# A gather ring that shrinks from seven slots to six at gather 301, with one head's query weights kept in the freed slot

## The reference, cut to what matters

```python
x = x + concat[retention(n(x)), short_conv(n(x))] @ w_out
x = x + peer(n(x));   y = rmsnorm(x)

def peer(x):                                  # per token, 8 heads
    q = (x @ wq).reshape(T, 8, 2, 128)        # wq: 1024 x 2048, 1 MB for each head
    s1, s2 = q[:, :, 0] @ keys1, q[:, :, 1] @ keys2        # 128 scores each
    v1, i1 = top_k(s1, 16); v2, i2 = top_k(s2, 16)
    top_s, sel = top_k(v1[..., :, None] + v2[..., None, :], 16)
    eidx = (i1 * 128 + i2)[sel]               # 16 of 16384 experts
    gate = softmax(top_s)
    act = gelu(x . u_tab[eidx])
    return sum(gate * act * v_tab[eidx])
```

## Time and profile before

| | |
|---|---|
| time, median of 3 runs | 2945.81 us |
| the profiled execution's own time | 2945.65 us |
| its span | 2943.8 us |
| around the span (the difference) | 1.85 us |
| DMA read and written | 1205.73 MB, mean 410 GB/s |
| of it the gathers' queue (q0) | 1107.36 MB |
| of it SyncE's queue (q1) | 95.93 MB |
| PE / DVE / ACT / POOL busy | 78% / 71% / 67% / 42% of the span |

### The profile page before, as it was taken

The page is one execution under the profiler, slowest core; times in us unless marked ns, Lnnn a source line. Parts: engine busy times, 40 slices in busy tenths (PEclk is TensorE's granted clock), DMA queues, the critical chain, the costliest instruction groups (busy, mean ns, idle before and its releaser), DMA issues.

```text
span 2943.8 us, 36236 instructions
## 1 busy us (share of the span) xinstructions
PE 2300.3 (78%) x12548; PEld 1804.2 (61%) x12548; DVE 2077.0 (71%) x5143; ACT 1967.8 (67%) x3670; POOL 1240.7 (42%) x1063
## 2 busy tenths in 40 slices
PE   9989898998777768888986887778766667666677
PEld 8878786665555556666665555555555555555555
DVE  3677788675688787777666555788868788865544
ACT  2477666777677677666667776777767666667663
POOL 0234334444334334433344344344454445455553
PEclk9999999999888878999996989898866656766669
DMA  8899999999999999999999999999999999999998
GB/s 340 318 403 404 420 408 411 412 420 420 420 419 417 412 410 404 421 421 419 418 418 404 419 420 421 412 420 418 411 419 410 420 420 416 403 414 416 422 421 361
DMA packets 182055, 1205.73 MB, mean 410 GB/s; under 512 B 21744, under 2 KB 27184, under 8 KB 43504
## 3 DMA queue, kind: packets, MB, share of 16 engines
q0 software_dynamic: 152368, 1107.36, 91.2%
q1 hardware_dynamic: 29264, 95.93, 8.3%
q10 hardware_dynamic: 240, 0.13, 0.0%
HBM read 1198.48 MB, written 4.86 MB: 409 GB/s over the span
## 4 chain that ended last, share of the span: by engine, by line
DMA 38%; DVE 24%; PE 22%; ACT 10%; issue 4%; POOL 1%; DVEq 0%; SPq 0%; ACTq 0%; POOLq 0%
DMA ring<-in_uv,idx 38%; DVE ring L2014 12%; PE expert_sum L1590 9%; ACT ring L1210 5%; PE x_ps L1371 2%; PE mm L1473 2%; ACT weights L1206 1%; POOL ring L950 1%; PE mm L1276 1%; DVE pairs_left L1819 1%; DVE pairs_left L1938 1%; ACT L1190 1%; ACT dots L1190 1%; PE expert_sum L1276 1%; PE x_ps L1276 1%
## 5 line engine op out<-in xcount | busy, mean ns | idle before, releaser
L950 POOL DMA_INDIRECT ring<-in_uv,idx x1054 | 1235.1, 1172 | 1683.8 <-PE expert_sum L1590 1464.1
L1590 PE MATMUL expert_sum<-ident_sb,ring 128*128 128x128 f32 x8192 | 1356.6, 322 | 594.5 <-ACT ring L1210 587.8
L2014 DVE CUSTOM_DVE_ANT_0 ring<-ring,xn 128x1024 f32<-128x1024 f32 x1056 | 1285.0, 1222 | 656.8 <-DMA ring<-in_uv,idx 646.8
L1590 PEld LDWEIGHTS expert_sum<-ident_sb,ring 128*128 128x128 f32 x8192 | 1130.2, 167 | 893.4 <-ACT ring L1210 827.6
L1210 ACT ACTIVATE ring<-ring,weights 128x1024 f32<-128x1024 f32 x1024 | 1176.2, 1149 | 33.3
L1190 ACT ACTIVATE dots<-dots 128x1 f32<-128x1 f32 x1056 | 211.5, 200 | 798.7 <-DVE dots L2014 792.2
L1206 ACT ACTIVATE weights<-dots,gate 128x1 f32<-128x1 f32 x1024 | 301.7, 295 | 37.1
L1473 PE MATMUL mm<-xn_in,stream 128*128 128x416 f32 (+1 forms) x500 | 198.3, 521 | 0.0
L1276 PE MATMUL mm<-stream,xn_in 128*128 128x256 f32 (+1 forms) x640 | 162.0, 387 | 0.0
L1276 PEld LDWEIGHTS mm<-stream,xn_in 128*128 128x128 f32 (+1 forms) x640 | 103.9, 177 | 21.4 <-issue 3.8
L1473 PEld LDWEIGHTS mm<-xn_in,stream 128*128 128x128 f32 x500 | 89.9, 200 | 39.6 <-issue 25.1
(11 more groups left out here) (397 smaller groups left out, 1955.6 us busy)
## 6 DMA issues: line engine op xcount, KB each, us to landing
stream<-in_wq SPq DMA_DIRECT2D x21, 1024.0 KB
ring<-in_uv,idx POOLq DMA_INDIRECT x1054
stream<-in_w_conv SPq DMA_DIRECT2D x16, 1024.0 KB
stream<-in_w_ret SPq DMA_DIRECT2D x16, 1024.0 KB
ring<-in_w_ret SPq DMA_DIRECT2D x6, 1024.0 KB, 12.4
x<-in_x SPq DMA_DIRECT2D x8, 512.0 KB, 10.0
out_y<-xn SPq DMA_DIRECT2D x8, 512.0 KB
stream<-in_w_out SPq DMA_DIRECT2D x3, 1024.0 KB
```

The source lines that it names most:

```text
L950: pool.indirect_dma_start(ring[:, g % RING, :], None, uv, bass.IndirectOffsetOnAxis(ap=rows, axis=0)).then_inc(landed[g % RING], 16)
L1590: ins = pe.matmul(expert_sum[:, c * P:(c + 1) * P], ring[:, g % RING, D + c * P:D + (c + 1) * P], ident_sb[:, :], is_transpose=True, start ...
L2014: dve.tensor_tensor_reduce(u, u, xn[:, t % 2, :], 1.0, 0.0, ALU.mult, ALU.add, dots[:, g % RING:g % RING + 1]).then_inc(dotted, 1)
```

## The change: six slots, one kept weight, and works moved

From gather 301 on (`SMALL_RING` = 43 x 7) the gathers go round slots 0 to 5. `slot_of`, `lap_of` and `same_slot_before` replace `g % RING`, `g // RING` and `g - RING` everywhere. The seventh slot is loaded once with the two halves of head 7's query weights, and the pass of head 7 of groups 1 and 2 reads them there, so these two passes leave `STREAM` (60 entries before, 58 now).

Beside it works move: the four x of group 2 are loaded at gather 301 instead of 333; their squares stand at 319, 328, 337 and 346 instead of 346, 348, 350 and 352; the root at a tile's end stands 6 gathers behind it instead of 3 (but for tiles 0, 3 and the sample); the exponentials of tile 3's last four heads stand at 364 instead of 356; the sample's choices start at 853 and are 13 gathers apart instead of 856 and 9. The number of instructions is the same but for the two streamed loads that go and the one that comes.

```diff
-LATER_AT = {4: (374, 11), 6: (654, 16), 7: (775, 10), SAMPLE: (856, 9)}
+LATER_AT = {4: (374, 11), 6: (654, 16), 7: (775, 10), SAMPLE: (853, 13)}
+SMALL_RING = 43 * RING
+def slot_of(g):
+    return g % RING if g < SMALL_RING else (g - SMALL_RING) % (RING - 1)
+def lap_of(g):
+    return g // RING if g < SMALL_RING else SMALL_RING // RING + (g - SMALL_RING) // (RING - 1)
+def same_slot_before(g):
+    return g - RING if g < SMALL_RING + RING - 1 else g - RING + 1
...
-    return {2: 40, 3: 45, 4: 48}.get(t, first_use_at(2) - 7 + 4 * place(t))
+    return {2: 41, 3: 45, 4: 48}.get(t, first_use_at(2) - 7 + 4 * place(t))
...
-    return {0: mix_at(2) + 16}.get(t, end_of(t) + 3)
+    return {0: mix_at(2) + 16, 3: end_of(3) + 3, SAMPLE: TOTAL + 3}.get(t, end_of(t) + 6)
...
-ON_CHIP = {... if p[2] == (0,) or p[2] == (1,) and p[1] in (2, 3)}
+ON_CHIP = {... if p[2] == (0,) or p[2] == (1,) and p[1] in (2, 3) or p[0] and p[1] == PH - 1}
...
+def exp_at(t, last):
+    return choose_at(last, t) + {(0, 3): 5, (3, 7): 14}.get((t, last), 6)
...  # load_x_ahead
-                yield mix_at(1) + 20 if t == 4 else first_use_at(j) - (26 if t < 5 else 32)
+                yield mix_at(1) + 20 if t == 4 else first_use_at(j) - (26 if t < 5 else 64)
...  # load_consts, SyncE
+                yield SMALL_RING + 1
+                sp.wait_ge(slot_free, SMALL_RING)
+                sp.dma_start(ring[:, RING - 1, :].rearrange("p (b k n) -> p b k n", b=2, k=KC),
+                             wq[2 * PH - 2:2 * PH].rearrange("b p k n -> p b k n")).then_inc(kept_wq_in, 16)
...  # GpSimd
-                    pool.wait_ge(slot_free, g - RING + 1)
+                    pool.wait_ge(slot_free, same_slot_before(g) + 1)
...  # norm, ScalarE
-                yield x_root_at(t) - (0 if t < 2 else (8, 6, 3)[place(t)] if t < 5 else 9 - 2 * place(t))
+                yield x_root_at(t) - (0 if t < 2 else (8, 6, 3)[place(t)] if t < 5 else 36 - 9 * place(t))
...  # queries, TensorE
-                    if m in ON_CHIP and h > 1:
+                    if m in ON_CHIP and j:
+                        pe.wait_ge(kept_wq_in, 16)
+                        weight = [chunks_of([ring[:, RING - 1, s * D:(s + 1) * D]]) for s in range(2)]
+                    elif m in ON_CHIP and h > 1:
```

More of the change, by code:

```diff
@@ L168 @@
     PASSES += [(j, h, GROUPS[j], last_turn_at(j) + 5 + PASS_EVERY * h, 2, 0) for h in range(PH)]
-ON_CHIP = {n: p[1] for n, p in enumerate(PASSES) if p[2] == (0,) or p[2] == (1,) and p[1] in (2, 3)}
+ON_CHIP = {n: p[1] for n, p in enumerate(PASSES) if p[2] == (0,) or p[2] == (1,) and p[1] in (2, 3) or p[0] and p[1] == PH - 1}
 SCORED = {(2, 3, 4): [(2, 0), (4, 2), (3, 7)], (5, 6, 7, SAMPLE): [(5, 0), (7, 2), (SAMPLE, 4), (6, 7)],
@@ L949, in _ @@
                 rows = idx[:, QUADS_IN if t == SAMPLE else t % 5, k:k + 1]
-                pool.indirect_dma_start(ring[:, g % RING, :], None, uv,
-                                        bass.IndirectOffsetOnAxis(ap=rows, axis=0)).then_inc(landed[g % RING], 16)
+                pool.indirect_dma_start(ring[:, slot_of(g), :], None, uv,
+                                        bass.IndirectOffsetOnAxis(ap=rows, axis=0)).then_inc(landed[slot_of(g)], 16)
         @block.scalar
@@ L1122, in exponentials @@
                     n = rows_of(t)
-                    yield choose_at(last, t) + (5 if (t, last) == (0, 3) else 6)
+                    yield exp_at(t, last)
                     act.wait_ge(exp_in, pick(last, t) + 1)
@@ L1182, in _ @@
                 t, k = tile_of(g)
-                d = dots[:, g % RING:g % RING + 1]
+                d = dots[:, slot_of(g):slot_of(g) + 1]
                 if t == SAMPLE and k == 0:
@@ L1204, in _ @@
                 act.wait_ge(gelu_done, g + 1)
-                w = weights[:, g % RING:g % RING + 1]
+                w = weights[:, slot_of(g):slot_of(g) + 1]
                 act.activation(w, d, ACT.Copy,
@@ L1579, in _ @@
                         pe.wait_ge(last_v_in[0], 16)
-                        spread_sum(spread[:, k % 3, :], P, ring[:, g % RING, D:], False, False, range(0, 2))
+                        spread_sum(spread[:, k % 3, :], P, ring[:, slot_of(g), D:], False, False, range(0, 2))
                         pe.wait_ge(last_v_in[1], 16)
-                        spread_sum(spread[:, k % 3, :], P, ring[:, g % RING, D:], False, False,
+                        spread_sum(spread[:, k % 3, :], P, ring[:, slot_of(g), D:], False, False,
                                    range(2, QUADS)).then_inc(slot_free, 1)
@@ L1637, in norm @@
                 dve.wait_ge(x_rooted, r + 1)
+                dve.wait_ge(x_scaled, 2 * r)
                 op(dve.reciprocal(stat[0:n, 9:10], stat[0:n, 10 + place(t):11 + place(t)]))
@@ L1950, in gates @@
                     n, heads = rows_of(t), last - first + 1
-                    yield choose_at(last, t) + 8
+                    yield max(exp_at(t, last) + 3, choose_at(last, t) + 8)
                     dve.wait_ge(exp_done, b + 1)
@@ L2011, in _ @@
                         dve.wait_ge(xn_placed, t - 1)
-                dve.wait_ge(landed[g % RING], 16 * (g // RING + 1))
-                u = ring[:, g % RING, 0:D]
+                dve.wait_ge(landed[slot_of(g)], 16 * (lap_of(g) + 1))
+                u = ring[:, slot_of(g), 0:D]
                 dve.tensor_tensor_reduce(u, u, xn[:, t % 2, :], 1.0, 0.0, ALU.mult, ALU.add,
-                                         dots[:, g % RING:g % RING + 1]).then_inc(dotted, 1)
+                                         dots[:, slot_of(g):slot_of(g) + 1]).then_inc(dotted, 1)
                 advance(programs, g)
```

22 lines of the change are left out of this document (11 added, 11 removed).

## The result

The changed kernel takes 2959.68 us (median; 2958.02 to 2966.92), the kernel before beside it 2946.82 (2943.51 to 2950.26): a ratio of 1.0045, 95% interval 1.0034 to 1.0056. The forecast was 2969 us in 2940 to 2990, slower. The profiled execution has a span of 2957.2 us, 13.4 more than before.

What follows compares the result with a forecast made beforehand. The prediction took the gathers' DMA bytes, at 421 GB/s in quiet stretches, to bound the kernel. Its terms, -2.5 + 31 + 10 + 8 - 23 = +23.5 us on 2945.65, gave 2969 us, range 2940 to 2990.

Steps and rivals of the forecast that it cites:

- The bytes: Head 7's weights: two 1 MB loads go and one comes, at 421 GB/s: -2.5 us.
- The quiet round: Gathers without delays, six slots: round 14.9 us, work on a slot 5.3, issue to landing 9.6, rate 421 GB/s kept.
- The table switches: ScalarE's two table loads around an exponential or root, 28 behind 950 us: 28 + 13 us, three quarters taken, +31 us.
- the edge: Shortest time from a gather's issue to its landing that loses nothing: about 8.8 us, allowing 6.1 us of work without stream.
- the three quarters of the prediction: Share of table-switch delays counted, since some late gathers land on VectorE's free time: 31 us kept.
- Other delays and the restart: TensorE and VectorE delays 10 us, losses in present dips beside table loads 8 us, minus today's 23 us loss.
- The moves: Works spread at group 2's x and tile ends thin out piled delays; already in the sum, +15 us at most if they fail.
- the 23 us: Present loss from 950 to 2900 us, in short dips: 416 GB/s against 421 in quiet stretches.
- The signs: Changed profile: 2400 to 2450 us near 400 GB/s, 420 or 421 slices with switches near 415, VectorE and ScalarE waits grow.
- Five in flight are enough: Six slots: issue to landing can shrink to 5.7 us without loss; 2939 or 2944 us; chance 0.30.
- Every delay costs its full period: Six slots: 2.49 us for each of 28 table switches and 10 other places; 2990 us, +92 at most; chance 0.14.
- The kept load: Head 7's weights in the seventh slot might arrive late, stalling TensorE at gathers 330 and 713; 2945 to 2950 us; chance 0.01.

Runs made afterwards that it cites:

- experiment 4: The kernel before, with head 7's two passes reading another resident array, so two 1.05 MB loads go (wrong choices): 2940.86 us, ratio 0.9980.
- experiment 6: The changed kernel (six slots) with exponentials and roots behind gather 295 replaced by operations needing no table load (wrong values): 2945.64 us, ratio 1.0000.
- experiment 7: The changed kernel with seven slots, head 7's weights streamed, and late exponentials and roots replaced by copies and sums: 2944.87 us, ratio 0.9993.
- experiment 1: The changed kernel with seven slots to the end and head 7's weights streamed as before, leaving only the moved works: 2946.26 us, ratio 0.9997.
- experiment 10: The longer switches: the changed kernel with one more table load and root behind each of 15 exponentials: 2980.77 us, ratio 1.0124.
- experiment 2: The changed kernel with all moved works put back; six slots and kept weights stay: 2961.44 us, ratio 1.0047.
- experiment 5: The changed kernel with five slots from gather 301 in place of six: 3115.65 us, ratio 1.0571.

## Why the prediction was right, and where its sum was off

The sum said +23.5 us and it was +13 (12.9 by the medians, 13.4 by the spans). By its steps:

- **The bytes, -2.5.** Measured -2.8 (experiment 4). DMA bytes are the 1204.7 MB predicted.
- **The quiet round.** 14.9, 5.3 and 9.6 us at 422 GB/s, as predicted: a slot less costs nothing where nothing delays.
- **The table switches, +31.** This term was mis-sized. The cause is the right one: taking the switches away takes 14.0 us from six slots (experiment 6) and 1.4 from seven (experiment 7), so 12.6 of the 13.4 us between the kernel of experiment 1 and the changed one hang on them. But 28 of them cost 14.0, not 31. The step that failed is the edge: 8.8 us, read from one dip that lost 1.1 us. The earlier trace rows has that dip; at that place seven slots have 399 GB/s even without a switch, 391 and 406 with one (the table above), so much of the dip isn't the switch's, and it is no measure of an edge. Five slots show an average of 8.3. With that, and the 5.3 + 2.86 = 8.2 us of work instead of my 8.4, the excess is 8.2 - (14.94 - 8.3) = 1.6 us in stretches without stream and 8.2 - (16.4 - 8.3) = 0.1 in those with it. At the three quarters of the prediction this is 12 x 1.2 + 16 x 0.1 = 16 us, where 14.0 were measured; the windows have 0.95 for the 1.2. This sum was made after the result and no run tested it by itself. That the switches under the stream cost next to nothing is worked out, (14.0 - 12 x 0.95)/16 = 0.16 us each, and wasn't measured by itself. The longer switches fit it: of their 21.1 us the last five took 5 x (2.2 - 0.95) = 6, so the ten before them took 1.5 us each for 1.5 us more, as they would if they stood just at the edge.
- **Other delays and the restart, 10 + 8 - 23 = -5.** Without switches six slots are 0.8 us above seven although they move one load less, so 0.8 + 2.8 = 3.6 us are what all other delays cost through the slot. Each of these two times is known to some 2.6 us (their intervals), so the 3.6 may be nothing or twice as much. The prediction replaced the whole loss of today by a new sum, and most of that loss stayed: even without a switch seven slots keep 416 GB/s behind 950 us, so it isn't the switches'. Whether an eighth slot would win it back wasn't run. One reading behind this term was wrong too: the issue at 1604.32 us in the earlier trace rows came late with no releaser, and not because of TensorE (see the last section).
- **Luck.** The switches were put 18 us too high (31 where they make 12.6 of the difference), and the rest 9 too low (-5 for 3.6). They have nothing to do with each other, and the second cancelled about half of the first; with the first alone the forecast would have been 2978 us.
- **The moves.** They were to thin out the piles in the 23 us. With seven slots they bring 0.2 us, with six at most some 2. The stretch at 1100 us did go from 387 to 406, as predicted, and it is 387 again where they are undone (experiment 2), but its 2 us don't show in the time.
- **The signs.** VectorE waits longer for gathers, as predicted. Of the five slices between 1180 and 2080 us that stood at 420 or 421 one fell to 409 and two by 2 or 3, and two stayed, so this sign came only in part; others fell more (419 to 406). ScalarE's wait for dots was to grow and didn't (557.0 to 558.8 us). The fall of 2400 to 2450 us came about, and experiment 1 shows it to be no evidence.
- **The rivals.** "Five in flight are enough" fell with experiment 5: with five slots the average flight in the quiet stretch was 8.3 us at 394 GB/s. Single flights did shrink to 6.44 us, but not all of them, as this rival wanted. By the Trainium skill's rule ("DMA: Bandwidth & Descriptors", section "Anatomy of one DMA — SWDGE (gpsimd) path") of 2.0 us and the bytes at 436 GB/s, an estimate of 4.4 us, five slots would have lost nothing; the runs are against its use for gathers that follow each other. "Every delay costs its full period" fell too: 0.5 us each. But something like it holds past the edge, where experiment 10 pays 1.4 us for 1.5. The kept load came in time: SyncE issued it at 957.94 us and it landed 12.7 us later, before the pass at gather 330.

In one line: seven slots 2946.3 (experiment 1); no switches 2944.9; the sixth slot with the kept weights, still without switches, 2945.6; with the switches 2959.7. Even with no switch at all the trade would only be even: one load is worth 2.8 us and the slot costs about 3.6. No run here that computes the right result is clearly faster than the kernel before.

What stays open: why a lone late issue costs 0.95 us where its excess over the edge is 1.6, and what makes up the better part of the 23 us that were lost with seven slots too, switches or none.

## What to carry to other kernels

The depth of a ring isn't judged in its quiet stretches, where a slot less costs nothing, but by the longest absence of any engine that works on a slot: here seven slots hid 2.86 us and 4.4 us nearly wholly, and six hid neither. Past the edge each further microsecond was paid almost in full, so a slot and a stall are traded against each other: taking a slot is only cheap once the stalls are gone. Find the edge by running with too few slots, not by reading one dip; a single stretch of 50 us varies by some 10 GB/s between kernels of the same time.

## What the runs showed of the hardware that was not expected

GpSimd now and then issues a gather late without anyone to wait for. Timeline of the kernel of experiment 1, transposes and issues:

```profile
2157.93 1.73 POOL L973 DMA_INDIRECT ring<-in_uv,idx  x1 [1.93 <-PE expert_sum L1616]
...
2158.16 1.97 PE L1616 MATMUL expert_sum<-ident_sb,ring 128*128 128x128 f32 x8 [0.51 <-ACT ring L1233]
2160.41 0.94 POOL L973 DMA_INDIRECT ring<-in_uv,idx  x1 [0.75 <-PE expert_sum L1616]
...
2160.65 1.97 PE L1616 MATMUL expert_sum<-ident_sb,ring 128*128 128x128 f32 x8 [0.52 <-ACT ring L1233]
...
2164.38 1.18 POOL L973 DMA_INDIRECT ring<-in_uv,idx  x1 [3.04 <-issue]
```

The transposes at 2158.16 end at 2160.13, and the issue follows 0.28 us later. Those at 2160.65 end at 2162.62, and the issue comes 1.76 us later, with no releaser. The changed kernel has the same behind transposes that end at 2410.04 and at 2686.27:

```profile
2408.07 1.97 PE L1620 MATMUL expert_sum<-ident_sb,ring 128*128 128x128 f32 x8 [1.37 <-ACT ring L1237]
...
2411.82 1.94 POOL L977 DMA_INDIRECT ring<-in_uv,idx  x1 [3.90 <-issue]
...
2684.30 1.97 PE L1620 MATMUL expert_sum<-ident_sb,ring 128*128 128x128 f32 x8 [1.50 <-ACT ring L1237]
...
2688.05 1.70 POOL L977 DMA_INDIRECT ring<-in_uv,idx  x1 [3.57 <-issue]
```

These two are 2688.05 - 2411.82 = 276 us or 108 gathers apart. Each such issue is 1.5 us late, which may be a part of the loss that neither switches nor slots explain; that wasn't measured. Its cause wasn't looked for.

The kernel before has them too, at 424.47, 725.33, 1013.26, 1302.16 and 1604.32 us, 107 gathers from one to the next. The last is the row that the prediction read as a delay by TensorE; the transposes before it:

```profile
1600.59 1.97 PE L1590 MATMUL expert_sum<-ident_sb,ring 128*128 128x128 f32 x8
```

They end at 1602.56, and the issue comes 1.76 us later.
